# Padding the feature tiles of the projections' activations: 16 different distances to the weights

## What is computed

```python
h = rms_norm(x, norm1_w);  proj = h @ w_in                # 2048 -> 5648
x = x + jnp.concatenate([attn, ssm], axis=-1) @ w_out     # 2048 -> 2048
h = rms_norm(x, norm2_w)
u = causal_dwconv(h @ w_up, ffn_conv_w, ffn_conv_b)       # 2048 -> 11264
u_gate, u_val = jnp.split(u, 2, axis=-1)
x = x + (jax.nn.silu(u_gate) * u_val) @ w_down            # 5632 -> 2048
...
proj = jnp.einsum('bsd,df->bsf', h, w_in)                 # second layer, 2048 -> 7168
out = jnp.einsum('bsf,fd->bsd', y, w_out)
return x + gate[:, None] * out
```

## The kernel before, in words

| tensor | address before | modulo 256 | address after | modulo 256 |
|---|---|---|---|---|
| whi (4 x 4096) | 49152 | 0 | 49152 | 0 |
| wlo (4 x 4096) | 65536 | 0 | 65536 | 0 |
| gh, tile kt | 81984 + 1024 kt | 64 | 81920 + 1056 kt | 32 kt mod 256 |
| gl, tile kt | 98368 + 1024 kt | 64 | 98816 + 1088 kt | 64 kt mod 256 |
| ah, al | 163008, 167104 | 192 | 164416, 168512 | 64 |
| wdt_h, column 16 kt | 164416 + 64 kt | 64 + 64 kt | 165824 + 64 kt | 192 + 64 kt |

## Time and profile before

### The profile page before, as it was taken

How to read it: one execution, slowest core, us unless ns; L and a number is a source line. 1 busy time by engine, 2 the same in 40 slices (tenths; PEclk the granted TensorE clock), 3 DMA queues, 4 the chain that set the end, 5 groups by cost and what they waited for, 6 DMA issues and landing times.

```text
span 1659.8 us, 33703 instructions
## 1 busy us (share of the span) xinstructions
PE 1607.7 (97%) x13254; PEld 1577.9 (95%) x13254; DVE 1160.1 (70%) x1357; ACT 807.0 (49%) x972; POOL 26.2 (2%) x53
## 2 busy tenths in 40 slices
PE   6999999999999999999999999999799999999997
PEld 6998899989999999999999999999799999999996
DVE  5776678675668888888888888576664544664755
ACT  6444345544554545545455454444455544444542
POOL 0000000000000000000000000000000000000000
PEclk9999999999999999999999999999999999999998
DMA  8454344455548777787787876555455555455451
GB/s 326 130 176 140 127 148 142 144 197 176 186 153 331 262 281 291 252 299 260 269 293 257 303 265 210 184 189 189 152 178 187 184 189 166 139 165 168 163 178 52
DMA packets 85043, 336.17 MB, mean 203 GB/s; under 512 B 9440, under 2 KB 9696, under 8 KB 78560
## 3 DMA queue, kind: packets, MB, share of 16 engines
q1 hardware_dynamic: 77328, 281.34, 49.6%
q0 software_dynamic: 7056, 51.38, 8.4%
q10 hardware_dynamic: 576, 2.24, 0.4%
HBM read 332.82 MB, written 2.10 MB: 202 GB/s over the span
## 4 chain that ended last, share of the span: by engine, by line
PE 72%; DVE 5%; issue 2%; ACT 1%; DVEq 0%; ACTq 0%
PE PS L1086 23%; PE PS L1088 23%; PE PS L1090 23%; DVE ada_w L921 1%; DVE wlo L577 1%; ACT whi L253 1%; PE PS L1188 1%; DVE UV L879 1%; PE PS L1155 1%; PE PS L1332 0%; DVE X L1073 0%; PE PS L1174 0%; DVE X L593 0%; DVE rb L611 0%; PE PS L1133 0%
## 5 line engine op out<-in xcount | busy, mean ns | idle before, releaser
L1086 PE MATMUL PS<-gh,whi 128*128 128x256 f32 x3520 | 999.5, 284 | 20.2 <-DVE wlo L577 15.1
L1088 PE MATMUL PS<-gl,whi 128*128 128x256 f32 x3520 | 985.7, 280 | 0.0
L1090 PE MATMUL PS<-gh,wlo 128*128 128x256 f32 x3520 | 984.0, 280 | 0.0
L577 DVE TENSOR_TENSOR wlo<-raw,whi 128x1024 fp32r<-128x1024 f32 x528 | 644.9, 1224 | 430.7 <-ACT whi L253 429.4
L253 ACT ACTIVATE whi<-raw 128x1024 fp32r<-128x1024 f32 x528 | 557.2, 1058 | 728.8 <-PE PS L1090 727.5
L1086 PEld LDWEIGHTS PS<-gh,whi 128*128 128x128 f32 x3520 | 664.6, 189 | 27.9 <-issue 24.7
L1088 PEld LDWEIGHTS PS<-gl,whi 128*128 128x128 f32 x3520 | 664.1, 189 | 2.8 <-issue 1.9
L1090 PEld LDWEIGHTS PS<-gh,wlo 128*128 128x128 f32 x3520 | 663.1, 188 | 0.0
L1086 PE MATMUL PS<-ah,whi 128*128 128x256 f32 x704 | 197.2, 280 | 11.0 <-DVE UV L879 7.3
L1088 PE MATMUL PS<-al,whi 128*128 128x256 f32 x704 | 195.8, 278 | 0.0
L1090 PE MATMUL PS<-ah,wlo 128*128 128x256 f32 x704 | 195.7, 278 | 0.0
(11 more groups left out here) (186 smaller groups left out, 803.1 us busy)
## 6 DMA issues: line engine op xcount, KB each, us to landing
raw<-weights SPq DMA_DIRECT2D x528, 512.0 KB, 3.4
ada_w<-w_ada POOLq DMA_DIRECT2D x48, 1024.0 KB, 5.3
X<-xT SPq DMA_DIRECT2D x4, 512.0 KB, 11.9
outT<-X SPq DMA_DIRECT2D x4, 512.0 KB, 2.6
c<-const ACTq DMA_DIRECT2D x1, 1536.0 KB, 6.4
c_act<-c_rows POOLq DMA_DIRECT2D x1, 1024.0 KB, 9.3
prm<-params SPq DMA_DIRECT2D x1, 276.5 KB, 3.8
mask<-const ACTq DMA_DIRECT2D x1, 256.0 KB, 9.4
```

Of the source, the lines that this page charges most:

```text
L577: dve.tensor_tensor(wlo[:, j % SPLIT, :], raw[:, j, :], whi[:, j % SPLIT, :].bitcast(F32), ALU.subtract).then_inc(s_lo, 1)
L1086: pe.matmul(out[:, t, :], whi[:, b, w], hi[:, kt, :], start=first and half == 0 and t % 2 == 0, stop=False, skip_group_check=True)
L1088: pe.matmul(out[:, t, :], whi[:, b, w], lo[:, kt, :], start=False, stop=False, skip_group_check=True)
L1090: mm = pe.matmul(out[:, t, :], wlo[:, b, w], hi[:, kt, :], start=False, stop=last and half == 1, skip_group_check=True)
```

## The change

Behind each feature tile of gh come 8 unused elements (32 bytes), behind each of gl 16 (64 bytes). The two paddings of 64 bytes, ahead of gh and behind gl, go. All that is placed behind gl (prm, cst, the work areas with ah, al, QKVZ, QB and so on) moves up by 1408 bytes. Every use of gh and gl goes through the views without the padding; PE's instructions and their order are the same, and on ACT and DVE those that write two tiles at a time (L366, L810) have the form 128x2x256 in place of 128x512.

```diff
--- before.py
+++ after.py
@@ -98,10 +98,9 @@
         raw, _ = place("raw", [P, RAW, 1024])
         whi, _ = place("whi", [P, SPLIT, 1024], F32R)
         wlo, _ = place("wlo", [P, SPLIT, 1024], F32R)
-        at[0] += 64
-        gh, _ = place("gh", [P, DT, S], F32R)
-        gl, _ = place("gl", [P, DT, S], F32R)
-        at[0] += 64
+        gh_padded, _ = place("gh", [P, DT, S + 8], F32R)
+        gl_padded, _ = place("gl", [P, DT, S + 16], F32R)
+        gh, gl = gh_padded[:, :, 0:S], gl_padded[:, :, 0:S]
         prm, _ = place("prm", [P, N_PARAMS])
         cst, _ = place("cst", [P, 3 * P + 32])
         rb, _ = place("rb", [P, S])
```

## The result

The changed kernel takes 1680.99 us (median of 4 runs, 1679.86 to 1682.35) against 1660.74 us (4 runs, 1660.25 to 1661.61): slower, at a ratio of 1.0121 with a 95% interval of 1.0105 to 1.0137. That is 20 us where 5 were forecast. The direction was right and the time lies in the stated range of 1638 to 1684, near its upper end; the size forecast was a quarter of the real one.

What follows compares the result with a forecast made beforehand. PE's time from one matmul's start to the next was taken to bound the kernel. 1661.47 us + 0.5 + 0.6 + 4.0 = 1666.6, with the runs' median 0.3 us lower: about 1666 us, range 1638 to 1684.

Steps and rivals of the forecast that it cites:

- The period is 256 bytes: In the 48 dt matmuls, whose distance to the weights changes by tile, intervals repeat every four tiles, 256 bytes.
- Term 1: 10,560 gh/gl matmuls: 117.2 ns each, as in the last 36 dt intervals, against 117.15 now; +0.5 us.
- rival D: gh/gl: each change of distance costs, +6.0 us, and distance 128, +8.4; with Term 2 +19 us, 1681; chance 0.20.
- Term 2: 2112 ah/al matmuls, moved from distance 192 to 64, mostly turn slow in the down projections: +0.6 and +4.0 us.
- Term 3: ACT and DVE writing gh and gl, two instruction groups now crossing a gap between tiles: no cost, 0 us.
- Rival B: gh/gl: distance decides cadence more strongly; half the distances behave like 192, -17.0 us, total 1649; chance 0.26.
- Rival C: Steadily changing distance breaks the slow cadence altogether: -40.7 us on gh/gl, -2.2 on ah/al, total 1620; chance 0.10.
- Rival E: PE's cadence is set by what came before, a wait or small matmul; distance is a bystander, 1661; chance 0.14.
- The formula with 109.2 ns: Matmul interval N/2.4 + 2.5 ns at N = 256; an estimate by it would be about 95 us saved.

Runs made afterwards that it cites:

- the fixed series: Against the kernel before: all moving tensors unpadded at one same distance from the weights modulo 256 bytes, one distance per kernel; 1642.55 to 1697.30 us.
- e1: Kernel before with gh and gl unchanged and 192 instead of 64 bytes behind gl, so ah/al lie at 64; 1664.05 us, ratio 1.0008.
- e2: Changed kernel with 128 bytes more behind gl, so ah/al stay at 192; 1680.87 us, ratio 1.0111 to the kernel before.
- e11: Kernel before with gh and gl both padded by 64 bytes a tile, ah/al at 64; 1668.99 us, ratio 1.0050.

## Why the prediction was right in direction and wrong in size

- **PE's start-to-start interval sets the end, and the distance takes part in it.** Right, and stronger than written: the fixed distances span 115.2 to 120.0 ns, 1642.55 to 1697.30 us.
- **The period is 256 bytes.** Right. The pattern after repeats every eight tiles, and in each kernel of the fixed series ah/al lie 256 bytes further than gh/gl modulo 1024, with the same mean to 0.3 ns.
- **Term 1, +0.5 us, is the step that failed.** It measured +14.7 us in PE's sum; counted as the term counts, 1.72 ns on 10,560 matmuls, it is +18. The term took 117.2 ns from the 36 dt intervals. These visit only multiples of 64 bytes, whose fixed prices average 117.8; the odd multiples of 32, which the text said occur nowhere in the trace, average 118.25, with 96 at 120.0. And the changed kernel gives high and low part of a tile different distances, which the dt matmuls too do in part, but with other pairs: 0.7 ns more. In the changed kernel the same last 36 dt matmuls take 118.9 ns each themselves. A rate taken from 36 intervals at the old distances was used for 10,560, where an error of 1 ns is 10 us. The range still held the time only because it was drawn wide enough for rival D; the forecast's own range, 1661 to 1671, did not.
- **Term 2, +4.6 us.** As a cadence right: ah/al at 117.8 ns throughout, in e1 by the shift alone. PE's sum over them rose by 4.0 us. As a part of the time it is not confirmed: undoing the shift (e2) left 1680.87 us, and the shift alone (e1) is not told from no change.
- **Term 3, 0.** Right: DVE busy 1161.0 us after, 1160.1 before; ACT 807.2 after, 807.0 before. For UV PE waits less.
- **Rival B** (half of the distances like 192) fell: of eight distances none but 192 favours 113.3. **Rival C** (113.3 nearly throughout) fell with the 118.88 ns of the changed kernel. **Rival E** fell with the fixed series, the same instructions in the same order at other cadences, and with the borders of e1.
- **Rival D** gave 1681 (its terms add up to 1680), which is what was measured, by parts that are mostly not the real ones. It charged 880 changes of tile 6 us, and e11 shows such changes for free; it held the distance 128 for the bad one, and tiles 2, 4 and 6 near 120, where 0 and 96 are the bad ones and the tiles 0 and 7 the dearest. That its sum met the measured time shows nothing for its parts.
- **The rule of the Trainium skill** ("SBUF — State Buffer", "Who interferes with whom": two independent read ports, and PE never waits on anyone), taken as the prediction takes it, would make all placings equal. The runs decide against it for this stream of matmuls: 1642.55 to 1697.30 us by placing alone.
- **The formula with 109.2 ns.** The Trainium skill ("TensorE: Matmul & The Clock Gate", "Back-to-back issue gap") gives it for the isolated gap of one matmul and says that in a stream of weight loads and matmuls both set the spacing. So it was no measure for this kernel, and neither is the estimate of 95 us; the fastest stretch in any run here has 113.3 ns.

## A version that beats both

e3, all moving tensors at 192, takes 1642.55 us: ratio 0.9882 (0.9866 to 0.9899) to the kernel before, 38 us below the changed one. It changes two numbers of the placing. Its gain is that about 250 units on gh/gl instead of 63 run near 113.3 ns: PE's sum over gh/gl falls from 1267.7 to 1247.5 us.

## What to carry to other kernels

Where a stream of matmuls bounds a kernel, measure its start-to-start interval, not the duration of one matmul, and try the offset between moving operand and weights as a parameter of one number: eight runs here found 3.3% between best and worst. Spreading the tiles over all offsets bought about the average of good and bad ones, and unequal offsets of high and low part cost something on top; here a fixed good offset for every moving tensor won. A padding also shifts everything placed behind it, so look at what else moves.

## What the runs showed of the hardware that was not expected

- f32r matmuls of 128x256, each with its own weight load, run at cadences that go with the distance of the two addresses modulo 256 bytes:

| distance | 0 | 32 | 64 | 96 | 128 | 160 | 192 | 224 |
|---|---|---|---|---|---|---|---|---|
| ns from start to start | 120.0 | 116.7 | 113.3 or 117.8 | 120.0 | 118.7 or 120.0 | 117.3 or 118.7 | 113.3 or 117.8 | 118.3 |

- The clock has no part in it: in the 384 intervals shown above it was granted in full in every one of these kernels (1.00 of the 2.4 GHz level).
- The weights' address counts as much as the moving tensor's: at equal distances the dt matmuls have equal intervals at seven different addresses, and moving the weights alone by 128 bytes shifts their sequence by two tiles.
- At 64 and 192 one of two cadences holds for hundreds of matmuls. That may be why e1 spreads from 1653 to 1667 us over ten executions, where the kernel at 0 has 1695.0 and 1695.6 in its two; one execution of each kernel has a trace, so this isn't shown.
- What in the chip makes the interval depend on the distance is not shown by any run here; only that it does.
